# Second mixer's attention: pairs of heads as one item instead of single heads

## The reference, cut to what matters

```python
def fox_attention(q, k, v, log_f):            # 8 heads of 64, blocks of 128 queries
    c = cumsum(log_f)                          # one forget sum per head and token
    s = einsum('bqhd,bkhd->bhqk', q_i, k) * d ** -0.5
    s = s + (c_i[..., :, None] - c[..., None, :])
    s = where(kpos <= qpos, s, NEG_INF)        # causal
    return einsum('bhqk,bkhd->bqhd', softmax(s), v)

def swa_attention(q, k, v, sinks, slopes):     # 8 query heads, 2 key heads of 64, window of 128
    s = s - slopes * dist;  s = where(in_window & blk_ok, s, NEG_INF)
    p = softmax(concatenate([s, sink]))[..., :-1]
    ...
def memory_attention(q, k, v):                 # 4 heads of 128 over 256 memory tokens
    p = softmax(einsum('bshd,bmhd->bhsm', q, k) * d ** -0.5)
    ...
def peer_ffn_2(h, ...):                        # the experts: 128 rows of u and of v for each token
    act = gelu(einsum('cd,ced->ce', h_c, u[e_c])) * g_c
    return einsum('ce,ced->cd', act, v[e_c])
```

## Time and profile before

| | us |
|---|---|
| median of 3 runs | 3988.92 (3985.97 to 3993.56) |
| the profiled execution: its own time | 3991.26 |
| its span, first to last instruction | 3989.4 |
| attention of half 0 | 1779 to 1948 |
| attention of half 1 | 2674 to 2860 |
| PE, DVE, ACT, POOL busy over the span | 77%, 59%, 23%, 29% |
| HBM read over the span | 1256 MB |

### The profile page before, as it was taken

The page is one execution under the profiler, slowest core; times in us unless marked ns, Lnnn a source line. Parts: engine busy times, 40 slices in busy tenths (PEclk is TensorE's granted clock), DMA queues, the critical chain, the costliest instruction groups (busy, mean ns, idle before and its releaser), DMA issues. The chain is left out here.

```text
span 3989.4 us, 51160 instructions
## 1 busy us (share of the span) xinstructions
PE 3057.4 (77%) x18686; PEld 1577.7 (40%) x18686; DVE 2370.5 (59%) x6158; ACT 915.4 (23%) x2506; POOL 1152.4 (29%) x1029
## 2 busy tenths in 40 slices
PE   5975596756787765988899865979798876676666
PEld 4853395612354211633455522634465531111111
DVE  6557745476446677457545577457645578655554
ACT  2113232012111112136321111136412111111111
POOL 0000000043333444323323342323333334444442
PEclk8998698867798876977999986969999987766666
DMA  5510002289999999988999997977999999999998
GB/s 214 188 68 1 6 4 93 97 364 400 350 384 372 419 411 393 400 322 309 367 398 373 370 406 269 411 286 264 348 416 376 360 398 395 413 419 417 420 420 354
DMA packets 207064, 1263.90 MB, mean 317 GB/s; under 512 B 25748, under 2 KB 28948, under 8 KB 72356
## 3 DMA queue, kind: packets, MB, share of 16 engines
q0 software_dynamic: 147456, 1073.81, 67.3%
q1 hardware_dynamic: 59368, 186.95, 12.6%
HBM read 1256.17 MB, written 4.46 MB: 316 GB/s over the span
## 5 line engine op out<-in xcount | busy, mean ns | idle before, releaser
L243 POOL DMA_INDIRECT held_z<-in_experts,held_expert x512 | 579.0, 1131 | 1274.6 <-PE held_acc L263 907.6
L263 PE MATMUL held_acc<-held_z,held_diag 64*64 64x512 f32 x4096 | 697.6, 775 | 286.8 <-ACT held_diag L289 262.9
L263 PE MATMUL held_acc<-held_pair,held_diag 64*64 64x512 f32 x4096 | 688.9, 768 | 253.8 <-ACT held_diag L289 248.9
L243 POOL DMA_INDIRECT held_pair<-in_experts,held_expert x512 | 569.6, 1112 | 1047.6 <-PE held_acc L263 971.4
L309 DVE CUSTOM_DVE_ANT_0 held_z<-held_z,held_hrow 128x1024 f32<-128x1024 f32 x512 | 625.5, 1223 | 377.4 <-DMA held_z<-in_experts,held_expert 371.1
L309 DVE CUSTOM_DVE_ANT_0 held_pair<-held_pair,held_hrow 128x1024 f32<-128x1024 f32 x512 | 625.4, 1223 | 369.3 <-DMA held_pair<-in_experts,held_expert 360.7
L289 ACT ACTIVATE held_diag<-held_bands,held_weight 128x64 f32<-128x64 f32 x1024 | 347.7, 340 | 1467.7 <-DVE held_weight L304 1434.3
L263 PEld LDWEIGHTS held_acc<-held_z,held_diag 64*64 64x64 f32 x4096 | 135.2, 157 | 693.3 <-ACT held_diag L289 566.4
L263 PEld LDWEIGHTS held_acc<-held_pair,held_diag 64*64 64x64 f32 x4096 | 134.3, 155 | 670.4 <-ACT held_diag L289 570.8
L282 ACT ACTIVATE held_bent<-held_dot 128x2 f32<-128x2 f32 x512 | 104.0, 203 | 716.1 <-DVE held_dot L309 688.7
L1773 PE MATMUL c_ps<-held_hT,c_w 128*128 128x256 f32 x640 | 151.9, 392 | 0.0
(11 more groups left out here) (499 smaller groups left out, 4038.8 us busy)
## 6 DMA issues: line engine op xcount, KB each, us to landing
pgh_w<-in_w_in SPq DMA_DIRECT2D x38, 512.0 KB
p2h_w<-in_w_in SPq DMA_DIRECT2D x36, 512.0 KB
p_raw<-in_w_in SPq DMA_DIRECT2D x34, 512.0 KB, 3.5
p_w_ada<-in_w_ada SPq DMA_DIRECT2D x16, 1024.0 KB, 6.1
c_w<-in_w_query SPq DMA_DIRECT2D x20, 512.0 KB, 3.2
held_z<-in_w_in SPq DMA_DIRECT2D x20, 512.0 KB
c_w<-in_w_peer_q SPq DMA_DIRECT2D x20, 512.0 KB
ada_w<-in_w_ada SPq DMA_DIRECT2D x4, 2048.0 KB, 18.7
```

The costliest lines, as they stand in the source:

```text
L243: pool.indirect_dma_start(self.pair[m % BUFS], None, self.layers[t // TT][0], bass.IndirectOffsetOnAxis(ap=self.expert[:, t % TT, s:s + 1] ...
L263: last = pe.matmul(self.sum_of(i)[to * BAND:(to + 1) * BAND], diag[band, :], up[band, turn * WIDE:(turn + 1) * WIDE], start=s == 0, stop=s ...
```

## The change

The second mixer calls a new function, `pair_attention_stage`, in place of `attention_stage` (which the first mixer keeps). An item is now a pair of heads for the same 128 queries: in half 0 N = 20 (8 fox, 8 swa, 4 mem), so 24 steps. In half 1 a fox head has 384 or 512 keys and two do not fit one bank; there fox heads stay single and N = 28 (16, 8, 4), 32 steps. `MIXER_LENGTHS` is not touched: the same 50 beats of each half are spread over 24 and over 32 points.

For a pair there is one bias, one maximum, one negation, one reciprocal, one transposed copy and one copy of the result, each over both heads; exponentials and scalings stay one for each head. The sink's exponential takes a subtraction on DVE (new line 1159) and one activation for both heads. A fox pair puts its two score blocks into both banks (`apart`), so the next item's scores wait for its exponentials. The products with values go to the upper and the lower 64 partitions of one bank, alternating between heads. DVE copies the result of item n-4 first in its step, no longer after the other two.

```diff
+        by_head = lambda ap, n: ap[:, 0:items[n].wide].rearrange("p (h n) -> p h n", h=items[n].count)
+        scores = lambda n: ps[:, :, 0:items[n].width] if items[n].apart else by_head(ps[:, n % 2, :], n)
...
+                def score(n):
+                    it = items[n]
+                    if n and (it.apart or items[n - 1].apart):
+                        pe.wait_ge(exped, n)
+                    elif n >= 2:
+                        pe.wait_ge(exped, n - 1)
...
+                    for o, (q, key, more) in enumerate(it.heads):
+                        last = pe.matmul(out[:, o, :], q, key, start=True, stop=more is None)
+                        if more is not None:
+                            last = pe.matmul(out[:, o, :], more[0], more[1], start=False, stop=True)
+                    last.then_inc(scored, 1)
...
+                    for o, j in [(o, j) for o in heads for j in range(keys)] if it.whole else [(o, j) for j in range(keys) for o in heads]:
+                        rows, column = it.lands[o]
+                        last = pe.matmul(po[rows, column * P:(column + 1) * P], it.values[o][j], pT[n % 2][:, (o * keys + j) * P:(o * keys + j + 1) * P],
+                                         start=j == 0, stop=j == keys - 1)
...
+                        for o in range(items[n].count):
+                            m = at[n] + o
+                            ins = act.activation(by_head(p[n % 3], n)[:, o, :], scores(n)[:, o, :], ACT.Exp, bias=nmax[:, m:m + 1],
+                                                 accum_out=total[:, m:m + 1])
+                        ins.then_inc(exped, 1)
+                        if sunken(n):
+                            act.activation(esink[:, sink_cols(n)], esink[:, sink_cols(n)], ACT.Exp).then_inc(sunk, 1)
...
+                    link(dve.reduce_max(nmax[:, cols(n)], got, AX))
+                    if sunken(n):
+                        link(dve.tensor_tensor(nmax[:, cols(n)], nmax[:, cols(n)], it.sinks, ALU.max))
+                        dve.tensor_tensor(esink[:, sink_cols(n)], it.sinks, nmax[:, cols(n)], ALU.subtract)
+                    dve.tensor_scalar(nmax[:, cols(n)], nmax[:, cols(n)], -1.0, None, ALU.mult).then_inc(maxed, 1)
...
+                    link(dve.reciprocal(inv[:, cols(n)], total[:, cols(n)]))
+                    for o in range(items[n].count):
+                        head = by_head(p[n % 3], n)[:, o, :]
+                        ins = dve.tensor_scalar(head, head, inv[:, at[n] + o:at[n] + o + 1], None, ALU.mult)
...
+                for step in range(N + 4):
+                    if 4 <= step:
+                        take(step - 4)
+                    if step < N:
+                        peak(step)
+                    if 1 <= step <= N:
+                        weigh(step - 1)
+                    beats.dve(dve, step)
...
-                for t, head in [(t, 2 * c + o) for t in tiles for o in range(2)]:
...
+                for t in tiles:
+                    for some in ([0, 1],) if t < 2 else ([0], [1]):
...
-            attention_stage(nc, own("foxa"), k, items, FH, FD, foxT, sunk_from=sunk_from, sinks=sinks, sunk_T=swaT, beats=beats["attention"], spare=spare,
...
+            pair_attention_stage(nc, own("foxa"), k, items, beats["attention"], spare, late_from, late_loads=[(mkv, memory)],
```

More of the change, by code:

```diff
@@ L2085, in second_mixer @@
             a = Room(nc, fox, own("fox"))
-            lanes = lambda head: slice(head % 2 * 64, head % 2 * 64 + 2)
+            lanes = lambda o: slice(o * 64, o * 64 + 2)
             items = []
+            both = lambda ap, count: bcast(ap, count, 1)
+            half_rows = [slice(0, FD), slice(FD, P)]
             for c in range(FH // 2):
-                for t, head in [(t, 2 * c + o) for t in tiles for o in range(2)]:
[L2090 to L2093, removed]
+                for t in tiles:
+                    for some in ([0, 1],) if t < 2 else ([0], [1]):
+                        part = [half_rows[o] for o in some]
+                        pair = [(z[half_rows[o], Y_FQ + c, here(t)], fox_k[half_rows[o], c, 0:(t + 1) * P],
+                                 (fq[lanes(o), c, here(t)], fk[lanes(o), c, 0:(t + 1) * P])) for o in some]
+                        rows = None if len(some) == 2 else part[0]
+                        items.append(Item(pair, both(k.causal[:], len(some)), [[v[:, c, j, half_rows[o]] for j in range(t + 1)] for o in some],
+                                          [(half_rows[o], 0) for o in some], foxT[rows if rows is not None else slice(0, P), c, here(t)], rows=rows, apart=len(some) == 2))
@@ L2094, in second_mixer @@
             kept = [(fox_k[:, :, 0:HALF], past.fox_k), (swa_k[:, 0:HALF], past.swa_k), (v[:, :, 0:HTILES, :], past.v)]
             alibi, sinks = a.sb("alibi", [P, SH, 2 * P]), a.sb("sinks", [P, SH])
[L2096 to L2100, removed]
+            for c in range(SH // 2):
+                part = half_rows[2 * c // (SH // SG)]
+                for t in tiles:
@@ L2101, in second_mixer @@
                     k0 = max(t - 1, 0)
-                    items.append((z[part, Y_SQ + head % 4, here(t)], swa_k[part, k0 * P:(t + 1) * P],
-                                  alibi[:, head, (0 if t else P):2 * P], [v[:, 4, j, part] for j in range(k0, t + 1)], head, t - first, None))
-            sunk_to = len(items)
+                    pair = [(z[part, Y_SQ + head % 4, here(t)], swa_k[part, k0 * P:(t + 1) * P], None) for head in (2 * c, 2 * c + 1)]
+                    items.append(Item(pair, alibi[:, 2 * c:2 * c + 2, (0 if t else P):2 * P], [[v[:, 4, j, part] for j in range(k0, t + 1)]] * 2,
+                                      [(half_rows[o], 0) for o in range(2)], swaT[:, c, here(t)], sinks=sinks[:, 2 * c:2 * c + 2]))
```

130 lines of the change are left out of this document (124 added, 6 removed).

## The result

The changed kernel takes 4002.0 us (median of 20 runs) beside 3990.5 us for the kernel before (20 runs on the same chips). The ratio is 1.0028, with a 95% interval of 1.0015 to 1.0040: about 11 us **slower**. The prediction was 3987 us and "within 0.2%"; that was wrong, and on the side of rival 3. The profiled execution took 4012.3 us. That is the slowest of the 20, so its 21 us over the profile of before overstate the difference.

A forecast was written before the change was run, and what follows sets the result against it. The gather bounds most of the kernel, but the attentions lie above that floor, with closed chains in two-slot steps. Half 0 +1 and half 1 -3 give -2 us on 3991.3, so 3989; the median lies 2.3 lower: 3987, range 3967 to 4009.

The forecast's parts named there:

- rival 3: Two-slot steps leave PE idle before the second slot, so the clock falls; fox 81, swa 66 us in half 0: 4013; chance 0.26.
- What bounds the kernel: Gather DMA bounds most of the kernel; the attentions, 168 and 182 us, lie above their 126 us floor, so savings there count.
- The chain: In two-slot steps peak, exponentials, copy, Gelu, diagonal, second slot and scores follow in turn: fox 7.5 us, swa 7.1 or 5.7.
- the list of what would show it: Half 0 fox and first swa steps 7 to 10 us, later swa near 6; clock under 0.65 for rival 3.
- Rival 2: Chains slip past each other, so all 29 us of saved DVE work appear: 3960 us; chance 0.09.
- The sum: Over both attentions: half 0 +1 us, half 1 -3 us, together -2 us on the profiled 3991.3.
- the clock in "Half 0": Fox at mean clock 0.70 takes 71 us against 68 (+3); swa at 0.83 takes 56 against 61 (-5).
- its deciding point: For rival 3: mean clock over fox and swa of half 0 at about 0.6 or lower.
- The early copy of the result: In mem of half 0 it ends a wait of PE, besides the merged passes; mem 21 us against 28 (-7).
- The tiling rule: Fox scores of two heads might overlap on different tiles, 4 us less in half 0; no overlap was taken.
- The chances: Whole kernel against 0.2% (8 us): faster 0.31, same 0.41, slower 0.28.

The follow-up runs named there:

- e2: Changed kernel, with ACT's whole first beat ahead of the exponentials in steps of two or more slots that begin with an even beat: 3939.6 us, ratio 0.9875.
- e5: Changed kernel, with DVE's result copy put back behind the maximum and the weighing: 4054.1 us, ratio 1.0166 to the kernel before.
- e7: Changed kernel, with three unread 128-column products on PE between its two slots in steps beginning with an even beat: 3977.2 us, ratio 0.9975.
- e12: Changed kernel, with only a fox pair's scores reordered: both heads' 64-row products, then both two-row products: 3984.3 us, ratio 0.9993 to the kernel before.
- e6: Kernel before, with DVE copying the result first in each step of the second mixer: 3977.1 us, ratio 0.9965.
- e10: e2 with a fox pair's scores reordered: both heads' 64-row products, then both two-row products: 3932.2 us, ratio 0.9845 to the kernel before.

## Why the prediction was wrong, step by step

**What bounds the kernel: right.** Over the kernels here the time moves with that of the attentions. From the changed kernel to e2 the attentions lose 56.6 us in the profiles and the ratios give 61; from before to e5 they gain 56, the ratios give 66.

**The chain: right.** Steps 8 to 10 of half 0 take 8.66, 8.24 and 8.66 us; the working gave 7.1 + 1.75 at the lower clock. The swa steps 12 to 15, with the Gelu last, take 6.17, 5.56, 5.43 and 5.27 (5.7 predicted, near 6 in the list of what would show it). Rival 2 (all of DVE's saved time appears) is refuted for the kernel as a whole; only swa of half 1, where DVE's sum had been the bound, shortened about as DVE did.

**The sum: each term within 3 us, and the four largest errors on one side.** Measured from first maximum to first maximum:

| part | predicted | measured |
|---|---|---|
| fox, half 0 | +3 | +5.3 (67.4 to 72.6) |
| swa, half 0 | -5 | -3.2 (61.1 to 57.9) |
| mem and drain, half 0 | +3 | +5.8 (40.0 to 45.8) |
| fox, half 1 | +14 | +16.9 (80.1 to 97.0) |
| swa, half 1 | -13 | -13.8 (62.6 to 48.9) |
| mem and drain, half 1 | -4 | -4.8 (39.9 to 35.0) |
| both attentions | -2 | +6.1 |

**The step that failed** is the clock in "Half 0": "A mean of 0.70 is 60% of the time at the lower: 8 / (0.6/10.1 + 0.4/7.5) = 71" and, for swa, "at 0.83 (34% low) 56". Both take the mean clock of the kernel before as that of the changed one, although the same text says that the new steps leave PE idle ahead of every second slot, and that the earlier trace rows shows the lower clock behind such idle time. Measured were 0.59 and 0.64. Rival 3 named this mechanism, and its deciding point, "about 0.6 or lower" over both parts. The two windows come to 0.61: at the point, and the 0.59 and 0.64 are under the 0.65 that the list of signs gives for rival 3. Its clock was right and its prices were too high: 81 and 66 us, where 72.6 and 57.9 were measured, so that the runs (4002) lie between forecast (3987) and rival 3 (4013). The Trainium skill's section on HAM oscillation ("TensorE: Matmul & The Clock Gate") was the rule that spoke against the change; e7 agrees with it: 0.59 to 0.74 in fox of half 0 when the wait is filled. It is not the whole account of the clock, as e12 shows, where PE waited longer at a higher clock. The price of a step at the lower clock was in its turn too high by some 3 us for the eight: by the formula 0.59 would give 76 for fox, measured were 72.6.

With the measured clocks the same two formulas give 76 for fox (+8) and 61 for swa (0), and the sum is +8, a loss as it was measured (+6.1) and not the gain that was forecast. That this comes so close is partly luck. The steps at the lower clock are priced some 3 us too high in each of the two parts; in mem with the drain of half 0 and in fox of half 1 the sum is 3 us too low in each. Those two were priced at the upper clock and measured at 0.87 (mem) and 0.83; whether the clock makes their 3 us isn't shown. As the forecast stands, the clock of half 0 is 4 of the 8 us that the attentions took beyond it (2.3 in fox, 1.8 in swa).

Of the 11 us that the runs show, the attentions of the two profiles account for 6. The other 5 stay open: in stages that the change doesn't touch, the profiled executions differ by as much among the kernels here (the stretch from `pg` of half 0 to the first maximum of half 1 takes 728 to 737 us in all of them).

**Two terms booked as one small one.** The early copy of the result was priced within mem alone ("ends a wait of PE for it"). It is worth 14 us to single heads (e6) and 55 us to pairs (e5). Since the change makes both edits at once, the true sum was -14 for the copy and +26 for the pairing; I had booked -2 without noticing that it consisted of two large terms of opposite sign.

**The tiling rule** of the Trainium skill ("TensorEngine Tiling (Array Packing)", Key Properties) that I had not let into the sum: in the order of the changed kernel the records come one after the other, so taking no overlap was right. In the other order the trace agrees with the rule: two tiles run side by side, and no drain is to be seen between the products of 64 rows and of two (whether these count as two modes isn't shown). My estimate of 4 us less was for the order as written, where it is 0; with the order changed it is 14 in the chain.

**The chances.** "Slower" had 0.28 and the range (3967 to 4009) holds 4002.

## What to carry to other kernels

When slower pacing puts two pieces of background work into one step, look at what the second piece's operand stands behind on the engine that makes it; moving that operand's making into a wait that exists anyway was worth 1.25% here, more than four times what the change lost. A saved instruction on an engine that isn't waited for gives nothing until such a chain is open: the same pairs lost 26 us with it and gained about 30 without it. And never take the mean clock of the kernel before for a changed order of PE's work: cost each step at both levels, and ask of each new wait of PE which level it leaves behind. That question is a warning and no formula: e12 had more waiting and a higher clock.

## What the runs showed of the hardware that I had not expected

- Added work on TensorE can make a kernel faster. 14.5 us of products that nobody reads, put into PE's wait in half 0, raised the granted clock of fox from 0.59 to 0.74 and, with their like in half 1, took 21 us off the kernel.
- The order of two heads' products decides whether they overlap: 64-row products for rows 0 to 63 and 64 to 127 next to each other take 0.63 us together, with a two-row product between them 0.63 each. The two-row products overlap in the same way.
- The clock in fox of half 0 ranged from 0.58 (e5) to 0.85 (e10) over kernels that do the same products there. In e12 it was 0.68 with PE idle for 16.1 of 60 us, in the changed kernel 0.59 with PE idle for 11.9 of 73 us.
